# A two-layer hybrid encoder trunk on one core: fewer and larger residual loads, transposes placed earlier between matmuls, and a rolled vector loop

## The chip, the cores and the metric

The kernel runs on one core of one Trainium2 chip. The metric is the device time of one execution in microseconds (us). Engines are named as the profile names them: PE (TensorE), DVE (VectorE), ACT (ScalarE), POOL (GpSimd) and SP (SyncE, which issues most of the loads). PSUM is written by PE and read by DVE and ACT.

## The reference

512 tokens of width 2048 pass a layer of mixer A and a layer of mixer B. Only what the change touches is shown; the last line of each layer, a 512x2048 by 2048x2048 product with a residual added, is where most of the changed lines stand.

```python
def layer_a(h, ...):
    u = rms_norm(h, g_norm)
    x_rnn, g_rnn, q_mem, g_mem = jnp.split(u @ w_in, ...)
    x_rnn = causal_depthwise_conv(x_rnn, conv_w, conv_b)
    y_rnn = rg_lru(x_rnn, ...) * jax.nn.silu(g_rnn)      # three turns of four blocks of 128 channels
    y_mem = memory_attention(q_mem, mem_k, mem_v) * jax.nn.silu(g_mem)
    return h + jnp.concatenate([y_rnn, y_mem], axis=-1) @ w_out

h = layer_a(x, ...)
k_sb, v_sb = jnp.split(rms_norm(h, kv_norm) @ w_kv, 2, axis=-1)
h = layer_b(h, ..., k_sb, v_sb, ...)                      # same shape, stick-breaking attention
return rms_norm(h, final_norm)
```

## The kernel before, in words

Every large product runs in fp32r as three passes (`three_passes`, L1666 to L1668): each operand is split into a high part, made by ACT, and a low part, made by DVE as the difference, and PE multiplies high by high, high by low and low by high. So each piece of weights that lands in SBUF goes landing, ACT (`w_hi`), DVE (`w_lo`), PE, and each engine's order is written out by hand with counting semaphores.

**Output projections.** `project(s, ...)` computes layer s's output product by Strassen's scheme with seven block products per half: 28 "halves" (u = 0 to 27), each of 24 matmuls with 512 columns, each on 1 MB of weights (`load_proj` on SP's queue, `proj_split` on ACT and DVE). ACT splits the weights of half u once half u-2 is done. While SP's queue brings the weights, ACT's queue brings the residual: `load_resid` in layer A reads x in four loads of 512 columns (1 MB each, issued behind the splits of halves 4, 7, 10 and 13), `load_h2` in layer B reads h in four such loads and the final gain in a fifth (behind 4, 7, 10, 12 and 14). DVE adds the residual to the products as they come out of PSUM.

**Transposes of h.** The next product, with `w_kv`, wants h transposed. Eight units q of eight 128x128 transposes each (`h_transposed(q)` on PE, L1720) write two PSUM banks; `h_fill(q)` on ACT (L541) and then on DVE (L1026) copy them out as high and low parts, after which `h_lo` counts the banks free. `H_UNITS` says which columns unit q takes, `h_unit` which banks. Units 0 to 3 share two banks and stand before halves 20, 21, 22 and 23; unit 4 stands in half 27; units 5, 6 and 7 stand in the first two slabs of the next product. A slab is four tiles of twelve matmuls; a hook `{t: f}` runs f before tile t. Unit 5 uses other banks than unit 4.

**The recurrent loop.** Layer A's input projection runs in three turns of two groups of four slabs. PE, ACT and SP run it as a rolled loop (`Fori`), DVE unrolled. DVE's part of slot 0 and 1 is the convolution (L1353, L1359) and the low part of its result (L1373), for which PE waits with the gates. ACT stores y at slot 7 (`store_y`, L658); DVE waits for that store in slot 3 of the next turn before it overwrites the tile.

**The end.** The last quadrants of layer B's product are added (`last_sum`, L1627), squared on ACT (L952), and each row of four tiles is scaled: ACT scales the left half (`row_scale`, L981), DVE the right half (`row_out`), and SP stores them. For rows 0 and 1, `row_out` multiplies chunk 3 by the gain and the scale in one instruction; for rows 2 and 3 the gain has been multiplied in earlier (`pregain`, L1561).

Of the kernel before, what the change touches and what calls it, by code (L numbers as in the profile page):

```python
# [19 lines left out]
P = 128  # L20
# [4 lines left out]
C = 512  # L25
# [5 lines left out]
NPAIR = NB // 4  # L31
# [4 lines left out]
CONV = 4  # L36
# [16 lines left out]
F_MEM, F_X = 0, 4  # L53
H_UNITS = ((0, 0), (0, 1), (1, 0), (1, 1), (3, 0), (2, 0), (3, 1), (2, 1))

# [6 lines left out]
ALU = mybir.AluOpType  # L62
# [41 lines left out]
def trunk(nc, x, x_t, mem, mem_t, gain_cols, chan_cols, w_mem_kv, w_in_a, w_rec_gate, w_in_gate,  # L104
# [23 lines left out]
    with ExitStack() as ctx:  # L128
# [3 lines left out]
        def sem(name):  # L132
            return ctx.enter_context(nc.semaphore(name))
# [72 lines left out]
        def h_rows(q, t, k):  # L206

            c, second = H_UNITS[q]
            at = P * (2 * second + k)
            return r_a[c // 2][:, t, c % 2, at:at + P]  # L210

        def h_unit(q):

            k0 = 4 * H_UNITS[q][0] + 2 * H_UNITS[q][1]
            banks = main[:, 0:2, :] if q < 4 else aux[:, 2 * (q % 2):2 * (q % 2) + 2, :]
            return slice(k0, k0 + 2), banks

# [82 lines left out]
        y_stored = sem("y_stored")  # L300
        resid_loaded = [sem(f"resid_loaded{c}") for c in range(4)]
        h_stored = sem("h_stored")
# [214 lines left out]
        def _(act):  # L517
# [275 lines left out]

            def load_resid(m):
                act.wait_ge(y_stored, 64)
                act.dma_start(r_a[m // 2][:, :, m % 2, :], x_v[:, :, C * m:C * m + C]).then_inc(resid_loaded[m], 16)

# [4 lines left out]
            def late_a(u):  # L802
                if u == 16:
                    act.wait_ge(r_done, 2)
                    act.wait_ge(psum_read, 7)
                    act.dma_start(h_v[:, :, 0:2 * C], r_a[0][:].rearrange("p t c n -> p t (c n)")
                                  ).then_inc(h_stored, 16)
                if u in (18, 20):
                    for t in (u - 18, u - 17):
                        if t:  # L810
                            act.wait_ge(h_squares, t)
                        nc.scalar.activation(work[:, 0:1024], r_a[0][:, t], ACT.Square, accum_out=ss[:, t, 1:2]
                                             ).then_inc(h_squares, 1)
                if u == 21:
                    h_fill(0)
                if u == 22:
                    h_fill(1)
                if u == 23:
                    h_fill(2)
                if u == 24:  # L820
                    h_fill(3)
# [6 lines left out]

            project(0, late_a, load_resid, (4, 7, 10, 13))
            extra[0] = N_PROJ  # L830
            act.wait_ge(r_done, 3)
            store_h(3)
            split(G_KV, 0, g_kv)
            h_fill(4)
            for j in range(4):
                split_next(G_KV, j, g_kv, g_kv)
                if j == 0:
                    store_h(2)
                    h_fill(5)
                    h_fill(6)  # L840
                if j == 1:
                    h_fill(7)
                    chunk_squares(3, 1)
                    chunk_squares(2, 2)
                if j == 2:
                    root(3)
# [128 lines left out]

            project(1, late_b, load_h2, (4, 7, 10, 12, 14))

# [19 lines left out]
        def _(dve):  # L997
# [340 lines left out]
            for b in range(4):  # L1338
                branch_out(G_A, b)
            for i in range(NPAIR):  # L1340
                for q in range(2):
                    G = 2 * i + (G_A + 1 + q)
                    for j in range(4):
# [31 lines left out]
                        if slot == 3:  # L1375
                            if i:
                                dve.wait_ge(y_stored, 16 * i)
                            for b in range(4):
                                gate_out(G, b)
# [16 lines left out]
                        if slot == 7:  # L1396
                            for b in range(4):
                                branch_out(G, b)
            mem_branch(0, G_A + 7, g_a)

            r11, r12, r21, r22 = project(0, r_a, lambda n: dve.wait_ge(resid_loaded[n], 16))

            for u in range(16, N_PROJ):
# [6 lines left out]
                if u == 18:  # L1410
                    dve.wait_ge(resid_loaded[3], 16)
                    fifth(0, r22, r12)
                if u == 21:
                    h_fill(0)
                    dve.wait_ge(resid_loaded[2], 16)
                    first_copy(0, r11)
                if u == 22:
                    h_fill(1)
                if u == 23:
                    h_fill(2)  # L1420
                    y_quad(0, 16, q_k1[1], 2)
                if u == 24:
                    h_fill(3)
                    second_sums(0, aux[:, 2:4, :])
# [12 lines left out]
            V.tensor_tensor(r21, main[:, 2:4, :], r21, ALU.add).then_inc(psum_read, 1)  # L1437
            h_fill(4)

            for j in range(4):  # L1440
                split_next(G_KV, j, g_kv, g_kv)
                if j == 0:
                    h_fill(5)
                    h_fill(6)
                if j == 1:
                    h_fill(7)
                if j == 2:
                    dve.wait_ge(h_squares, 12)
                    mean_square(4, ss[:, :, 1:4])
                    rstd_rows(3)  # L1450
# [161 lines left out]
            ch.link(V.reduce_sum(mx[:], ss[:, :, 0:3], AX_X))  # L1612
            ch.link(V.tensor_scalar(mx[:], mx[:], 1.0 / D, EPS, ALU.mult, ALU.add))

            def row_out(t):
                o = h2[:, t, 3, :]
                if t < 2:
                    V.scalar_tensor_tensor(o, o, rstd[:, t:t + 1], fgain[:, 3 * C:4 * C], ALU.mult, ALU.mult)
                else:
                    V.tensor_scalar(o, o, rstd[:, t:t + 1], None, ALU.mult)  # L1620
                o = h2[:, t, 2, :]
                V.scalar_tensor_tensor(o, o, rstd[:, t:t + 1], fgain[:, 2 * C:3 * C], ALU.mult, ALU.mult
                                       ).then_inc(scaled[1], 1)
# [37 lines left out]
        def _(pe):  # L1661
# [44 lines left out]
            def h_transposed(q):  # L1706
# [6 lines left out]
                else:  # L1713
                    pe.wait_ge(r_done, 3)
                    pe.wait_ge(psum_read, 12 if H_UNITS[q][0] == 3 else 14)
                    if q > 5:
                        pe.wait_ge(h_lo, q - 1)
                for k in range(2):
# [173 lines left out]
            half(0, 20, a23, 2, 0)  # L1892
            h_transposed(1)
            half(0, 21, a23, 2, 1)
            h_transposed(2)
            pe.wait_ge(p1_copied, 2)
            half(0, 22, a01, 3, 0)
            h_transposed(3)
            half(0, 23, a01, 3, 1)
# [10 lines left out]
            for j in range(4):  # L1910
                hooks = {}
                if j == 0:
                    pe.wait_ge(psum_read, 13)
                    hooks = {2: lambda: (pe.wait_ge(psum_read, 14), h_transposed(5)), 3: lambda: h_transposed(6)}
                if j == 1:
                    hooks = {1: lambda: h_transposed(7)}
                if j == 2:
# [109 lines left out]
```

## Time and profile before

| | |
|---|---|
| median of 3 runs | 1490.51 us (1490.11 to 1491.57) |
| the profiled execution | 1490.51 us, of which the span of instructions is 1488.8 us |
| PE busy | 1474.2 us, 99% of the span |
| DVE, ACT busy | 928.1 us (62%), 682.6 us (46%) |
| granted TensorE clock | 0.998 |
| DMA | 314.90 MB, mean 212 GB/s |

The span runs from the first to the last instruction; 1.7 us of the time lie around it. A matmul's end in the trace is modelled, so two matmuls overlap in it; the time from one start to the next is what one costs.

### The profile page before, as it was taken

The numbers are of one execution on the slowest core, as the hardware profiler recorded it, in microseconds if no ns is written. First come the engines' busy times: TensorE is split into PE (matmuls) and PEld (weight loads), VectorE is DVE, ScalarE is ACT, GpSimd is POOL, SyncE is SP. The second block draws the span as 40 slices with busy tenths as digits, with TensorE's granted clock in tenths as the row PEclk, the third lists the DMA queues.
The fourth block names the chain that finished last, engine by engine and source line by source line (L and its number), as shares of the span: only waits on it lengthen the run. The fifth ranks groups of instructions, "written<-read, shape, count | busy, mean of one in ns | idle before, by whom it ended". The sixth has DMA issues, their size and how long they took to land.

```text
span 1488.8 us, 18103 instructions
## 1 busy us (share of the span) xinstructions
PE 1474.2 (99%) x6754; PEld 1225.9 (82%) x6754; DVE 928.1 (62%) x1319; ACT 682.6 (46%) x1087; POOL 93.4 (6%) x140
## 2 busy tenths in 40 slices
PE   8999999999999999999999999999999999999997
PEld 7888888888888888888888888888888888888886
DVE  5764568465677896843433334556666566678877
ACT  5764454445445545552323222433443433555465
POOL 0001111111110000011111101100000000000000
PEclk9999999999999999999999999999999999999999
DMA  9786788777786986378877998883342433349853
GB/s 325 245 337 215 160 217 226 179 228 156 206 251 181 334 301 245 137 258 223 244 205 215 293 212 248 231 204 123 140 142 86 141 138 127 130 167 343 309 196 141
DMA packets 157753, 314.90 MB, mean 212 GB/s; under 512 B 6656, under 2 KB 36352, under 8 KB 154624
## 3 DMA queue, kind: packets, MB, share of 16 engines
q1 hardware_dynamic: 103312, 197.06, 37.8%
q0 software_dynamic: 23040, 67.12, 20.8%
q10 hardware_dynamic: 31344, 49.98, 9.6%
q8 instruction: 34, 0.56, 0.1%
q14 instruction: 23, 0.19, 0.0%
HBM read 284.77 MB, written 96.47 MB: 256 GB/s over the span
## 4 chain that ended last, share of the span: by engine, by line
PE 93%; DMA 2%; DVE 2%; ACT 1%; issue 0%; SPq 0%; ACTq 0%; DVEq 0%
PE main L1666 25%; PE main L1667 25%; PE main L1668 25%; PE aux L1666 5%; PE aux L1667 5%; PE aux L1668 5%; PE aux L1958 2%; DMA w_raw<-weight_sums 1%; PE aux L1947 1%; DMA y_scratch<-work 1%; PE aux L1789 0%; DMA w_raw<-in_w_mem_kv 0%; DVE w_lo L1013 0%; ACT w_hi L527 0%; ACT work L554 0%; DVE work L1240 0%
## 5 line engine op out<-in xcount | busy, mean ns | idle before, releaser
L1013 DVE SCALAR_TENSOR_TENSOR w_lo<-w_raw,gains,w_hi 128x512 fp32r<-128x512 f32 x412 | 282.3, 746 | 311.6 <-ACT w_hi L527 311.1
L1666 PE MATMUL main<-act_hi,w_hi 128*128 128x512 f32 x1216 | 475.7, 391 | 0.0
L1668 PE MATMUL main<-act_hi,w_lo 128*128 128x512 f32 x1216 | 473.8, 390 | 0.0
L1667 PE MATMUL main<-act_lo,w_hi 128*128 128x512 f32 x1216 | 473.6, 389 | 0.0
L527 ACT ACTIVATE w_hi<-w_raw,gains 128x512 fp32r<-128x512 f32 x412 | 264.1, 714 | 384.4 <-PE main L1668 324.7
L1668 PEld LDWEIGHTS main<-act_hi,w_lo 128*128 128x128 f32 x1216 | 228.2, 188 | 48.1
L1667 PEld LDWEIGHTS main<-act_lo,w_hi 128*128 128x128 f32 x1216 | 228.4, 188 | 46.6
L1666 PEld LDWEIGHTS main<-act_hi,w_hi 128*128 128x128 f32 x1216 | 228.3, 188 | 46.4
L1666 PE MATMUL main<-w_hi,act_hi 128*128 128x512 f32 x544 | 212.5, 391 | 2.2 <-DVE w_lo L1122 1.9
L1668 PE MATMUL main<-w_hi,act_lo 128*128 128x512 f32 x544 | 211.8, 389 | 0.0
L1667 PE MATMUL main<-w_lo,act_hi 128*128 128x512 f32 x544 | 211.7, 389 | 0.0
L1666 PEld LDWEIGHTS main<-w_hi,act_hi 128*128 128x128 f32 x544 | 102.1, 188 | 25.4 <-DVE w_lo L1122 3.5
L1668 PEld LDWEIGHTS main<-w_hi,act_lo 128*128 128x128 f32 x544 | 102.1, 188 | 21.2
L1667 PEld LDWEIGHTS main<-w_lo,act_hi 128*128 128x128 f32 x544 | 102.1, 188 | 20.9
L562 ACT ACTIVATE w_hi<-w_raw 128x1024 fp32r<-128x1024 f32 x64 | 64.3, 1052 | 79.1 <-issue 62.2
L1043 DVE TENSOR_TENSOR w_lo<-w_raw,w_hi 128x1024 fp32r<-128x1024 f32 x64 | 75.6, 1221 | 38.1 <-ACT w_hi L562 38.0
L1666 PE MATMUL aux<-w_hi,act_hi 128*128 128x512 f32 x224 | 87.8, 392 | 0.6 <-DVE w_lo L1043 0.6
L1667 PE MATMUL aux<-w_lo,act_hi 128*128 128x512 f32 x224 | 87.2, 389 | 0.0
L1668 PE MATMUL aux<-w_hi,act_lo 128*128 128x512 f32 x224 | 87.2, 389 | 0.0
L562 ACT ACTIVATE w_hi<-work 128x1024 fp32r<-128x1024 f32 x48 | 48.2, 1053 | 53.5 <-issue 48.6
L494 POOL DMA_DIRECT2D weight_sums<-in_w_out_b x48 | 37.6, 787 | 458.1 <-issue 226.5
L1043 DVE TENSOR_TENSOR w_lo<-work,w_hi 128x1024 fp32r<-128x1024 f32 x48 | 56.6, 1220 | 14.3 <-ACT w_hi L562 14.1
(238 smaller groups left out, 1401.3 us busy)
## 6 DMA issues: line engine op xcount, KB each, us to landing
w_raw<-in_w_in_a SPq DMA_DIRECT2D x32, 1024.0 KB, 7.3
w_raw<-in_w_in_b SPq DMA_DIRECT2D x32, 1024.0 KB, 6.4
weight_sums<-in_w_out_a POOLq DMA_DIRECT2D x48, 512.0 KB, 7.4
w_raw<-in_w_kv SPq DMA_DIRECT2D x24, 1024.0 KB, 7.5
weight_sums<-in_w_out_b POOLq DMA_DIRECT2D x48, 512.0 KB, 7.6
w_raw<-weight_sums SPq DMA_DIRECT2D x18, 1024.0 KB, 8.2
weight_sums<-weight_sums POOLq DMA_DIRECT2D x32, 512.0 KB, 7.4
w_raw<-in_w_mem_kv SPq DMA_DIRECT2D x15, 1024.0 KB, 5.2
```

Of the source, the lines that this page charges most:

```text
L494: pool.dma_start(dst[rows], src[rows], accum_op=op).then_inc(sums_made[n], 16)
L527: nc.scalar.activation(w_hi[:, j % 2, k, :], w_raw[:, j % 2, k, :], ACT.Copy, scale=s).then_inc(hi_ready, 1)
L562: nc.scalar.activation(w_hi[:, u % 2, k:k + 2, :], proj_raw[RAW[u]][:, k:k + 2, :], ACT.Copy).then_inc(hi_ready, 2)
L1013: ins = V.scalar_tensor_tensor(lo, w_raw[:, j % 2, k, :], gain[:, KS * j + k:KS * j + k + 1], hi, ALU.mult, ALU.subtract)
L1043: V.tensor_tensor(w_lo[:, u % 2, k:k + 2, :], proj_raw[RAW[u]][:, k:k + 2, :], w_hi[:, u % 2, k:k + 2, :].bitcast(F32), ALU.subtract).then ...
L1666: TE.matmul(o, a[0], b[0], start=first, stop=False)
L1667: TE.matmul(o, a[0], b[1], start=False, stop=False)
L1668: return TE.matmul(o, a[1], b[0], start=False, stop=final)
L1947: last = TE.transpose(o, beta[:, t, c:c + P], ident[:])
L1958: last = TE.matmul(aux[:, 0, P * k:T], v, w, start=(k, n) == order[0], stop=(k, n) == order[-1])
```

## The change

It does six things. Unit q of the transposes takes the chunks in pairs (`CHUNK`), and unit 5 now writes the banks of unit 4, unit 6 the other two. On PE, unit 2 moves from before half 22 into the middle of half 21, unit 3 into the middle of half 22, unit 5 from tile 2 to tile 1 of the next product's first slab, unit 6 from tile 3 to tile 2, and unit 7 from tile 1 to tile 0 of the second; the fills follow. The fill of unit 4 moves behind the weight split of the next slab on ACT and on DVE. The residual x is read in two loads of 1024 columns (2 MB each), behind the splits of halves 4 and 5. The loads of h and the gain go out behind halves 4, 6, 8, 10 and 12. DVE's recurrent loop is rolled, with the wait for the y store at the end of slot 7 of the same turn. At the end, the gain of chunk 3 of rows 0 and 1 is multiplied in beforehand by two more instructions.

```diff
@@ -51,7 +51,7 @@
...
 F_MEM, F_X = 0, 4
-H_UNITS = ((0, 0), (0, 1), (1, 0), (1, 1), (3, 0), (2, 0), (3, 1), (2, 1))
+CHUNK = (0, 0, 1, 1, 3, 3, 2, 2)
@@ -205,15 +205,16 @@
...
-            c, second = H_UNITS[q]
-            at = P * (2 * second + k)
+            c = CHUNK[q]
+            at = P * (2 * (q % 2) + k)
             return r_a[c // 2][:, t, c % 2, at:at + P]
...
-            k0 = 4 * H_UNITS[q][0] + 2 * H_UNITS[q][1]
-            banks = main[:, 0:2, :] if q < 4 else aux[:, 2 * (q % 2):2 * (q % 2) + 2, :]
-            return slice(k0, k0 + 2), banks
+            k0 = 4 * CHUNK[q] + 2 * (q % 2)
+            banks = (main, main, main, main, aux, aux, aux, aux)[q]
+            b = (0, 0, 0, 0, 0, 0, 2, 0)[q]
+            return slice(k0, k0 + 2), banks[:, b:b + 2, :]
@@ -298,7 +299,7 @@
...
         y_stored = sem("y_stored")
-        resid_loaded = [sem(f"resid_loaded{c}") for c in range(4)]
+        resid_loaded = [sem("resid_loaded0"), sem("resid_loaded1")]
         h_stored = sem("h_stored")
@@ -791,9 +792,10 @@
...
-            def load_resid(m):
+            def load_resid(n):
                 act.wait_ge(y_stored, 64)
-                act.dma_start(r_a[m // 2][:, :, m % 2, :], x_v[:, :, C * m:C * m + C]).then_inc(resid_loaded[m], 16)
+                act.dma_start(r_a[n][:].rearrange("p t c n -> p t (c n)"), x_v[:, :, 2 * C * n:2 * C * n + 2 * C]
+                              ).then_inc(resid_loaded[n], 16)
@@ -815,9 +817,8 @@
...
                     h_fill(1)
+                    h_fill(2)
                 if u == 23:
-                    h_fill(2)
-                if u == 24:
                     h_fill(3)
@@ -826,16 +827,16 @@
...
-            project(0, late_a, load_resid, (4, 7, 10, 13))
+            project(0, late_a, load_resid, (4, 5))
             extra[0] = N_PROJ
...
             split(G_KV, 0, g_kv)
-            h_fill(4)
             for j in range(4):
...
                     store_h(2)
+                    h_fill(4)
                     h_fill(5)
@@ -973,7 +974,7 @@
...
-            project(1, late_b, load_h2, (4, 7, 10, 12, 14))
+            project(1, late_b, load_h2, (4, 6, 8, 10, 12))
@@ -1337,7 +1338,8 @@
...
                 branch_out(G_A, b)
-            for i in range(NPAIR):
+            with dve.Fori(0, NPAIR) as i:
+                ch.enter(i, 2 * (2 + 2 * (CONV - 2)) + 2 + 6)
                 for q in range(2):
@@ -1373,8 +1375,6 @@
...
                         if slot == 3:
-                            if i:
-                                dve.wait_ge(y_stored, 16 * i)
                             for b in range(4):
@@ -1396,9 +1396,11 @@
...
                                 branch_out(G, b)
+                            dve.wait_ge(y_stored, 16 * i + 16)
+                ch.leave(NPAIR)
             mem_branch(0, G_A + 7, g_a)
-            r11, r12, r21, r22 = project(0, r_a, lambda n: dve.wait_ge(resid_loaded[n], 16))
+            r11, r12, r21, r22 = project(0, r_a, lambda n: dve.wait_ge(resid_loaded[0], 16))
@@ -1408,19 +1410,18 @@
...
                 if u == 18:
-                    dve.wait_ge(resid_loaded[3], 16)
+                    dve.wait_ge(resid_loaded[1], 16)
                     fifth(0, r22, r12)
...
                     h_fill(0)
-                    dve.wait_ge(resid_loaded[2], 16)
                     first_copy(0, r11)
...
                     h_fill(1)
+                    h_fill(2)
                 if u == 23:
-                    h_fill(2)
                     y_quad(0, 16, q_k1[1], 2)
+                    h_fill(3)
                 if u == 24:
-                    h_fill(3)
                     second_sums(0, aux[:, 2:4, :])
@@ -1435,11 +1436,11 @@
...
             V.tensor_tensor(r21, main[:, 2:4, :], r21, ALU.add).then_inc(psum_read, 1)
-            h_fill(4)
...
                 if j == 0:
+                    h_fill(4)
                     h_fill(5)
@@ -1611,13 +1612,12 @@
...
             ch.link(V.tensor_scalar(mx[:], mx[:], 1.0 / D, EPS, ALU.mult, ALU.add))
+            pregain(3, 0)
+            pregain(3, 1)
...
                 o = h2[:, t, 3, :]
-                if t < 2:
-                    V.scalar_tensor_tensor(o, o, rstd[:, t:t + 1], fgain[:, 3 * C:4 * C], ALU.mult, ALU.mult)
-                else:
-                    V.tensor_scalar(o, o, rstd[:, t:t + 1], None, ALU.mult)
+                V.tensor_scalar(o, o, rstd[:, t:t + 1], None, ALU.mult)
                 o = h2[:, t, 2, :]
@@ -1712,9 +1712,9 @@
...
                     pe.wait_ge(r_done, 3)
-                    pe.wait_ge(psum_read, 12 if H_UNITS[q][0] == 3 else 14)
-                    if q > 5:
-                        pe.wait_ge(h_lo, q - 1)
+                    pe.wait_ge(psum_read, 12 if q < 6 else 14)
+                    if q > 4:
+                        pe.wait_ge(h_lo, (5, 0, 6)[q - 5])
                 for k in range(2):
@@ -1890,12 +1890,9 @@
...
             half(0, 20, a23, 2, 0)
-            h_transposed(1)
-            half(0, 21, a23, 2, 1)
-            h_transposed(2)
+            half(0, 21, a23, 2, 1, lambda t: h_transposed(1 + t))
             pe.wait_ge(p1_copied, 2)
-            half(0, 22, a01, 3, 0)
-            h_transposed(3)
+            half(0, 22, a01, 3, 0, lambda t: h_transposed(3) if t else None)
             half(0, 23, a01, 3, 1)
@@ -1911,9 +1908,10 @@
...
                     pe.wait_ge(psum_read, 13)
-                    hooks = {2: lambda: (pe.wait_ge(psum_read, 14), h_transposed(5)), 3: lambda: h_transposed(6)}
+                    hooks = {1: lambda: h_transposed(5),
+                             2: lambda: (pe.wait_ge(psum_read, 14), h_transposed(6))}
                 if j == 1:
-                    hooks = {1: lambda: h_transposed(7)}
+                    hooks = {0: lambda: h_transposed(7)}
                 if j == 2:
```

## Rows read from the trace of the kernel before

**Rows 1.** The page: busy us, share of the span, instructions.
```profile
PE 1474.2 (99%) x6754; PEld 1225.9 (82%) x6754; DVE 928.1 (62%) x1319; ACT 682.6 (46%) x1087; POOL 93.4 (6%) x140
```

**Rows 2.** Chain that ended last, us 494 to 510: start, us, what.
```profile
495.94 9.15 DMA w_raw<-weight_sums
...
506.38 1.24 DVE w_lo L1043
...
507.66 0.50 PE aux L1666
```

**Rows 3.** SP's and ACT's issues, by time: start, us, engine, line.
```profile
496.48 0.53 SPq L422 DMA_DIRECT2D work<-in_w_out_a  x1
...
498.02 0.39 ACTq L796 DMA_DIRECT2D work<-in_x  x1
```

**Rows 4.** DMA, us 496.4 to 496.8: issues, KB each, us to landing.
```profile
work<-in_w_out_a SPq DMA_DIRECT2D x1, 1024.0 KB, 13.1
```

**Rows 5.** DMA queues, us 502 to 508: packets, MB, share of 16 engines.
```profile
q1 hardware_dynamic: 672, 1.32, 58.6%
q10 hardware_dynamic: 520, 1.03, 45.2%
```

**Rows 6.** DMA queues, us 1393 to 1395.
```profile
q10 hardware_dynamic: 244, 0.50, 66.0%
q1 hardware_dynamic: 248, 0.25, 36.5%
```

**Rows 7.** DMA queues, us 564 to 571: a store of 4 KB rows on q10.
```profile
q10 hardware_dynamic: 523, 2.08, 74.9%
```

**Rows 8.** Chain, us 586 to 660: the transposes.
```profile
595.95 0.87 PE main L1720 x8
...
602.29 0.87 PE main L1720 x8
...
634.20 0.87 PE aux L1720 x8
```

**Rows 9.** ACT and DVE by time, around the second fill.
```profile
597.95 1.01 ACT L541 ACTIVATE act_hi<-main 128x1024 fp32r<-128x1024 f32 x1
...
599.50 1.22 DVE L1026 TENSOR_TENSOR act_lo<-main,act_hi 128x1024 fp32r<-128x1024 f32 x1
```

**Rows 10.** DVE by time, around the fifth fill.
```profile
637.86 1.23 DVE L1437 TENSOR_TENSOR work<-main,work 128x1024 f32<-128x1024 f32 x1 [2.85 <-PE main L1668]
...
640.13 2.73 DVE L1013 SCALAR_TENSOR_TENSOR w_lo<-w_raw,gains,w_hi 128x512 fp32r<-128x512 f32 x4
```

**Rows 11.** ACT, DVE, PE by time, around the loop's third turn.
```profile
322.05 0.41 ACTq L658 DMA_DIRECT2D y_scratch<-work  x1
...
330.96 2.74 DVE L1013 SCALAR_TENSOR_TENSOR w_lo<-w_raw,gains,w_hi 128x512 fp32r<-128x512 f32 x4 [1.44 <-ACT w_hi L527]
...
339.64 1.28 DVE L1373 TENSOR_TENSOR xc_lo<-work,xc_hi 128x512 fp32r<-128x512 f32 x2
...
342.23 0.40 PE L1666 MATMUL aux<-xc_hi,gate_hi 128*128 128x512 f32 x1
```

**Rows 12.** DMA, us 322 to 322.5: issue, KB, us to landing.
```profile
y_scratch<-work ACTq DMA_DIRECT2D x1, 1024.0 KB, 9.5
```

**Rows 13.** DVE and ACT by time, at the end.
```profile
1468.38 1.28 DVE L1561 TENSOR_TENSOR work<-work 128x512 f32<-128x512 f32 x2
...
1476.20 0.68 DVE L1627 TENSOR_TENSOR work<-main,work 128x512 f32<-128x512 f32 x1
...
1479.82 0.69 DVE L1627 TENSOR_TENSOR work<-main,work 128x512 f32<-128x512 f32 x1 [0.79 <-PE main L1668]
...
1474.87 2.19 ACT L981 ACTIVATE work<-work,rstd 128x1024 f32<-128x1024 f32 x2 [1.03 <-DVE rstd L1648]
```

**Rows 14.** Stretches at the end: us, busy by engine, PEclk, DMA, GB/s.
```profile
1480.00:1483.70 3.70, 0.00 (x0) 0.00 (x0) 3.47 (x10) 2.38 (x5) 0.00 (x0) 1.00 1.02 402
1483.70:1488.80 5.10, 0.00 (x0) 0.00 (x0) 0.00 (x0) 0.00 (x0) 0.00 (x0) 0.50 0.71 283
```

## The prediction

> **What bounds the kernel now.** I read the page first: PE is busy for 1474.2 of the 1488.8 us of the span [rows 1], so only 14.6 us are not PE's, most of them ahead of the first product and behind the last. I take from this that a change which only relieves another engine can save nothing worth measuring, and that each microsecond for which PE newly waits is a microsecond of the time. So the question for every edit is whether PE arrives somewhere before what it needs. I then read the chain that ended last around layer A's output projection. It leaves PE there: the load for half 5 is issued at 495.94 and lands 9.15 us later, at 505.09; DVE's first low part ends at 507.62 and PE starts half 5 at 507.66 [rows 2]. So from landing to PE it takes 2.57 us, and half 5 has no slack at all. I read the transposes in the chain too: unit 1 at 595.95, unit 2 at 602.29, each 0.87 long [rows 8], so a half takes 602.29 - 595.95 - 0.87 = 5.47 us and a tile, half of it, 2.73 us. Then the times of DVE and ACT around the fills, the DMA queues, and the end.
>
> **The two large loads of x: +3.2 us (0 to 4.4).** Half 6's weights are issued at 496.48 and land 13.1 us later, at 509.6 [rows 3, 4]. PE starts half 6 at 507.66 + 5.47 = 513.1 and needs them landed by 513.1 - 2.57 = 510.5, so half 6 has 0.9 us of slack. The first load of x is issued at 498.02 [rows 3]; between 502 and 508 its queue moves 1.03 MB, the whole 1 MB load, beside 1.32 MB of weights, 2.35 MB in 6 us or 0.39 MB/us together [rows 5]. So I place the start of its traffic at 502, 4 us behind its issue, and there the weights still lack, at half the rate, 0.195 x 3.1 = 0.60 MB of half 5's load.
>
> How do two queues share? Where q1 moved rows of 1 KB and q10 rows of 2 KB, the packets were equal in number, 248 and 244, and the bytes 0.25 and 0.50 MB [rows 6]. So the packet is what is shared. Rows of 2 KB go as packets of 2 KB (520 for 1.03 MB [rows 5]) and rows of 4 KB as packets of 4 KB (523 for 2.08 MB [rows 7]). The new loads of x have 4 KB rows against weights of 2 KB, so I give the weights one third, 0.13 MB/us, while x is loading, and x two thirds, 0.26.
>
> The first x load then lasts from 502 to 510 (2.1 MB / 0.26), and the second, issued behind the split of half 5, follows at once or, if it too needs 4 us from an issue at about 507, at 511. Half 5's weights land at 502 + 0.60 / 0.13 = 506.6, 1.5 us late, and PE waits those 1.5 us. Half 6's 1.05 MB take 8.1 us more, to 514.7, or with the gap of 0.9 us between the x loads at 0.39 MB/us 1.8 us less, to 512.9. Against 510.5 that is 2.4 to 4.2 us late in all; the wait of half 5 is contained in it. I take 3.2. Half 7 comes through even: x ends at about 518, the weights of half 7 then have their last 0.5 MB at the full rate and land at 519.2, and PE starts half 7 at 513.1 + 3.2 + 5.47 = 521.8, which is 519.2 + 2.57. If it misses, it misses by tenths (upper end 4.4). The lower end is the equal share by bytes: then half 5 is as before and half 6's load lands at 505.1 + 1.05 / 0.195 = 510.5, just in time, for 0. The later loads of x fall away, but no half waited for weights there, so that gives nothing back. DVE's new wait for the first x load, ahead of half 7's split, is met when the load lands at about 510.5.
>
> The Trainium skill bears on this (DMA: Bandwidth & Descriptors, the table of terms under SWDGE vs HWDGE vs iDMA): a packet is preferably at most 4096 B and holds up to 64 descriptors, and the engine changes queue at packet boundaries. If rows of 2 KB were bundled up to 4 KB, the two queues would share by bytes and the sum would lack this term; by the rows above it has it.
>
> **Unit 2's transposes: +1.1 us.** They must wait until DVE has read unit 1 out of the shared banks. Before, ACT copies unit 1 from 597.95 and DVE from 599.50 to 600.72, and PE comes at 602.29 with 1.6 us to spare [rows 8, 9]. Now PE comes after unit 1 and one tile, at 595.95 + 0.87 + 2.73 = 599.55. Nothing in front of the two copies has moved, since ACT's and DVE's weight splits still precede them, so PE waits until 600.7: 1.15 us. Queued behind PE's wait is the rest of half 21; ACT's next split waits for that half and shifts with it. Unit 3 needs unit 2's copies: transposes end at 601.6, ACT 1.0 and DVE 1.2 more, 603.9, against PE at 600.7 + 0.87 + 5.47 = 607.0. No wait.
>
> **Unit 5's transposes: +2.4 us.** They now use unit 4's banks and come a tile earlier. Unit 4 starts at 634.20 [rows 8]; with its 0.87 and a tile of 2.73 the next slab starts at 637.8, and PE reaches the new place one tile later, at 640.5. What it needs is DVE's copy of unit 4, and that now stands behind the weight split. DVE adds from 637.86 to 639.1, and its four splits take 2.73 us [rows 10], to 641.75; the copy takes 1.22 [rows 9], to 642.9. PE waits 2.4 us. Had the copy stayed in front of the split, it would be 640.3 and the wait nothing; the order is what costs. Unit 6 has its own banks, unit 7 comes 9 us later; the slab behind has all its weights.
>
> **The end: +0.5 us (0 to 1.25).** The two extra multiplications, 1.28 us for a pair [rows 13], stand on DVE ahead of the scale that both ACT's first row scales (2.19 us from 1474.87) and the first `last_sum` (1476.20) wait for. ACT squares the sum right behind its row scales, so it is up to 1.25 us late; DVE's idle 0.79 us before the last sum at 1479.82 [rows 13] takes most of it. 1.25 - 0.79 is about 0.5; the cheaper scaling of two tiles gives back two or three tenths at most, off ACT's path.
>
> **The rolled loop: 0.** The new wait bites once: the y store issued at 322.05 takes 9.5 us, to 331.5, and DVE's next split started at 330.96, so 0.6 us. It is covered, since DVE's low part of the first block ends at half of 1.28 behind 339.64, 340.3, and PE comes for it at 342.23 [rows 11, 12]: 1.9 us of slack. What is left of it, 1.3 us, must hold any cost of values in registers, over some fourteen instructions.
>
> **The earlier loads of h: 0.** They stay 1 MB with 2 KB rows, one per two halves (10.9 us). At 0.39 MB/us all together a pair of halves wants 2 MB of weights and 1 MB of h, 3.15 MB or 8.1 us. The first, which falls on the tight half 5, is where it was. If that is wrong, its price is some tenths.
>
> **Sum.** 3.2 + 1.1 + 2.4 + 0.5 = 7.2 us. The profiled execution took 1490.51 us, which is the median of the runs as well, so no correction: 1497.7 us.
>
> **The rivals.** *Share by bytes (0.18).* The large loads cost nothing and the sum is 1490.5 + 4.0 = 1494.5. For it: rows of equal size share equally, so [rows 5] alone can't tell; against it [rows 6]. *Not slower (0.08): the copies are early.* The price of both transposes hangs on PE standing ahead of DVE; it vanishes if ACT and DVE have copied unit 1 by 599.5 and unit 4 by 640.5. With x also sharing by bytes this gives 1490.5 + 0.5 = 1491.0. Against it is that each copy is behind a split on two engines, and that 2.4 us don't fit into spare time of tenths. *The clock falls (0.06).* A wait of PE lets the granted clock drop from 2.4 to 1.2 GHz. The only drop in view is after the end: PE's last product is done before 1479.82 and the clock is 0.50 from 1483.7 on, over 5.1 us [rows 13, 14]. My longest wait is 2.4 us, shorter than those 3.9. Were the clock low for as long as 5.1 us after one wait, it would cost half, 2.6 us: 1500.3. The Trainium skill (TensorE: Matmul & The Clock Gate, HAM oscillation) warns that a DMA wait between groups of matmuls lets the array throttle again; no row here shows it within the work. *The rolled loop costs PE (0.04).* If each of the fourteen instructions took 0.15 us more, 2.1 + 0.6 - 1.9 = 0.8 us a turn, 2.4 for three: 1500.1.
>
> **How the numbers follow.** My sum keeps 0.62; 0.02 is left for a gain that I don't see. A difference under 0.2%, 3 us, is about what can't be told from no change. Even by bytes the sum is 4 us over. Slower takes 0.62 + 0.18 + 0.06 + 0.04 = 0.90, same 0.08, faster 0.02. The range leaves out the not slower case: from 1493.5 (by bytes, with the end at nothing and half a microsecond off the waits) to 1500.3, the upper ends of the loads and the end, or the clock.
>
> **What would show it.** In PE's waits: halves 5 and 6 waiting on `w_lo` for about 1.5 and 1.7 us, unit 2's transposes on `act_lo` for 1.1 and unit 5's for 2.4. Half 6's load landing at 513 to 515, with twice as many bytes as weights on ACT's queue from 502 on. DVE's turn of the loop 0.6 us later once. I am wrong if half 6's load lands by 511, if the transposes start without a wait, or if some half between 7 and 14 waits because DVE does not catch up.

## The result

The changed kernel takes 1501.68 us in the median of 6 runs, against 1490.93 us for the kernel before (6 runs on the same chips): a ratio of 1.0083, 95% interval 1.0062 to 1.0103. It is slower, by 10.7 us, and outside the predicted range. Its runs also spread, from 1500.56 to 1508.97 us, where those of the kernel before lie within 1.5 us. The execution with the profile took 1507.18 us with a span of 1505.5, so it is near the upper end of them, and the account below is of that one: 16.7 us. The median is not the time of such a run: with the profiled one there are seven, four between 1500.56 and 1501.77 us and three at 1505.24, 1507.18 and 1508.97.

The page (busy us, share of the span, instructions), which answers to [rows 1]:

```profile
PE 1479.1 (98%) x6754; PEld 1228.4 (82%) x6754; DVE 929.4 (62%) x1321; ACT 682.7 (45%) x1087; POOL 93.3 (6%) x140
```

PE has the same 6754 matmuls and 5 us more of busy time for them; the other 12 us are idle, nearly all of it waits. PE's waits (who waited for whom: us in total, times, longest us):

```profile
PE aux L1666 <- DVE w_lo L1044: 4.1, 4, 2.2
PE aux L1666 <- DVE mv_lo L1191: 3.4, 2, 3.1
...
PE aux L1720 <- DVE act_lo L1027: 2.5, 1, 2.5
...
PE main L1720 <- DVE act_lo L1027: 1.3, 1, 1.3
```

Three of the four rows were forecast: the weights' low parts around halves 5 to 7 (3.5 of the 4.1 us; the rest is half 5 of layer B, which waited 0.4 us before too), and the transposes of units 5 and 2. The second was not: 3.1 us in one wait for `mv_lo`, at the first head of layer A's memory attention, right behind the recurrent loop. Before, that group was 0.2 us. DVE, ACT and PE around it, by time (start, us, engine, line; in brackets the idle time before and what ended it), with the landing of ACT's issue:

```profile
416.14 0.41 ACTq L659 DMA_DIRECT2D y_scratch<-work  x1
...
422.93 0.69 DVE L1163 TENSOR_TENSOR work<-main,rstd_bc 128x512 f32<-128x512 f32 x1 [2.03 <-PE main L1668]
...
427.23 0.69 DVE L1197 TENSOR_TENSOR q_lo<-work,q_hi 128x512 fp32r<-128x512 f32 x1 [3.61 <-DMA y_scratch<-work]
...
428.74 0.36 PE L1666 MATMUL aux<-mk_hi,q_hi 128*128 128x256 f32 x1 [3.13 <-DVE mv_lo L1191]
```

```profile
y_scratch<-work ACTq DMA_DIRECT2D x1, 1024.0 KB, 10.9
```

ACT issues the third turn's y store at 416.14. It lands 10.9 us later, at 427.0. DVE has finished the turn at 423.6 and stands at the new wait for that store; in the kernel before it went straight on to the low parts of the first head. PE, which had 0.6 us in hand there, comes for them at 425.6 and gets them at 428.74.

The clock shows what becomes of the waits (stretch, us, PE, PEld, DVE, ACT, POOL busy with their counts, PEclk, DMA, GB/s), and PE's matmuls in the first of these stretches:

```profile
429.30:432.70 3.40, 3.40 (x15) 3.01 (x14) 2.56 (x5) 0.04 (x1) 0.77 (x1) 0.50 0.14 25
...
432.70:436.00 3.30, 3.30 (x16) 2.70 (x15) 3.27 (x8) 2.51 (x10) 0.16 (x1) 1.00 0.63 78
...
654.60:658.00 3.40, 3.40 (x14) 2.92 (x12) 0.84 (x1) 1.02 (x1) 1.72 (x3) 0.50 1.07 331
...
658.00:661.00 3.00, 3.00 (x19) 2.55 (x18) 0.38 (x1) 0.28 (x1) 0.00 (x0) 1.00 0.81 272
```

```profile
431.38 0.63 PE L1667 MATMUL main<-act_lo,w_hi 128*128 128x512 f32 x1
431.81 0.63 PE L1668 MATMUL main<-act_hi,w_lo 128*128 128x512 f32 x1
```

Twice the granted clock is at half, 1.2 GHz, for 3.4 us: from 429.3, behind the wait of 3.1 us, and from 654.6, behind unit 5's wait of 2.5 us. At half clock a matmul of 512 columns follows the last after 0.43 us, at the full 2.4 GHz after 0.23; so each fall costs half of 3.4, 1.7 us. The kernel before has no such stretch inside the work.

So the 16.7 us are: waits for weights 3.5, unit 2 1.3, unit 5 2.5, the memory head 3.1, two falls of the clock 3.4, the end 0.9, together 14.7. The rest is small: 0.8 us in the loop, 0.6 from first loads that land later, and the slower first matmul behind each wait.

### The profile page after: what moved, and what is told of

It is laid out like the page before. It is cut to its first block, busy times and chain, and to the rows that moved or that the text cites. A ratio compares the mean times of both kernels' runs of the same rounds, so it can differ in the third digit from the quotient of the medians.

```text
span 1505.5 us, 18338 instructions
## 1 busy us (share of the span) xinstructions
PE 1479.1 (98%) x6754; PEld 1228.4 (82%) x6754; DVE 929.4 (62%) x1321; ACT 682.7 (45%) x1087; POOL 93.3 (6%) x140
## 4 chain that ended last, share of the span: by engine, by line
PE 85%; DVE 6%; DMA 5%; ACT 2%; issue 1%; SPq 0%; DVEq 0%; ACTq 0%
PE main L1666 23%; PE main L1667 23%; PE main L1668 23%; PE aux L1666 4%; PE aux L1667 4%; PE aux L1668 4%; DMA y_scratch<-work 2%; PE aux L1956 2%; DMA work<-weight_sums 2%; DVE w_lo L1014 1%; DMA w_raw<-in_w_mem_kv 1%; PE aux L1945 1%; DVE w_lo L1044 1%; DMA w_raw<-weight_sums 1%; ACT w_hi L528 0%
```

## The experiments

Kernels named "changed" start from the changed kernel, the others from the kernel before. Each was timed in five rounds beside the kernel before. Medians are given with lowest and highest. The kernel before had medians of 1490.3 to 1490.6 us there.

**1. The loop as before (changed kernel).**

```diff
-            with dve.Fori(0, NPAIR) as i:
-                ch.enter(i, 2 * (2 + 2 * (CONV - 2)) + 2 + 6)
+            for i in range(NPAIR):
...
                         if slot == 3:
+                            if i:
+                                dve.wait_ge(y_stored, 16 * i)
...
-                            dve.wait_ge(y_stored, 16 * i + 16)
-                ch.leave(NPAIR)
```

> The changed kernel with DVE's recurrent loop as it was: unrolled, and the wait for the y store back in slot 3 of the next turn. Theory: what the prediction missed is the wait at the end of the third turn, where PE lost 3.3 us at the first memory head and then 3.4 us at half the clock (1.7 us). Then the PE wait on mv_lo (3.4 us in the changed kernel's profile) is 0.2 us as before, the clock drop behind it is gone, the two small gate waits of 0.3 us go as well, and the time is near the predicted 1497.7 us plus the 1.7 us of the second clock drop: 1498 to 1500, with a spread between runs below 2 us, where the changed kernel's was 8. Rival: the loss comes from somewhere else and this changes less than 1 us.

Measured: 1501.88 us (1501.25 to 1503.62), ratio 1.0077 (1.0064 to 1.0090). The wait on `mv_lo` is back at 0.2 us although this execution's third store took 9.2 us to land, and the spread is 2.4 us in place of 8.4. The median didn't fall: it was expected at 1498 to 1500 and is 1501.88, as the changed kernel's 1501.68. So the loop's change isn't what puts the changed kernel's median above the forecast; it makes the long runs. In this kernel's profile PE waits 3.5 us before halves 5 to 7, 1.3 and 2.5 us for units 2 and 5, the clock falls once (1.7 us), and the end is 1.2 us longer: 10.2 us. A load that landed late near 65 us, with a wait of 1.4 us, is why the profiled execution, 1503.21, is above the median. Why the median is about 2 us above what I expected isn't shown.

**2. The loop unrolled, with the late wait (changed kernel).** As experiment 1, but only the loop's head is put back; the wait stays at the end of slot 7.

```diff
-            with dve.Fori(0, NPAIR) as i:
-                ch.enter(i, 2 * (2 + 2 * (CONV - 2)) + 2 + 6)
+            for i in range(NPAIR):
...
-                ch.leave(NPAIR)
```

> The changed kernel with the loop unrolled again but the wait for the y store left at the end of slot 7. Theory (the wait's place is the cause): as the changed kernel, 1500 to 1507 us with a wide spread, DVE waiting on the y store in turns in which it lands late, PE waiting for mv_lo by up to 3 us. Rival (rolling the loop is the cause: values in registers, the branch): as the loop put back whole, 1498 to 1500, no wait on mv_lo.

Measured: 1507.36 us (1501.38 to 1510.22), ratio 1.0113 (1.0098 to 1.0128). The spread is back, 8.8 us, with the loop unrolled. So it goes with the wait's place and not with the rolling. The median is high because three of five runs are long ones, against three of seven of the changed kernel; the quickest runs are 1501.38 and 1500.56. The execution with the profile happened to be the quickest: its third store landed in 5.2 us, and PE's wait on `mv_lo` was 0.2. Its clock fell once, behind unit 5's wait (the two stretches with it):

```profile
647.00:650.00 3.00, 1.68 (x9) 1.71 (x10) 1.18 (x2) 0.00 (x0) 0.90 (x2) 0.74 0.96 295
650.00:653.00 3.00, 3.00 (x11) 2.40 (x11) 1.23 (x1) 1.02 (x1) 0.82 (x2) 0.69 1.01 323
```

This execution, 0.3 us below the changed kernel's median, shows what a run without the late store is made of: waits of 3.4 us before halves 5 to 7, 1.3 for unit 2, 2.5 for unit 5, 1.7 for the clock and 1.2 at the end are 10.1 of the 10.9 us by which its span is longer.

**9. The late wait alone (kernel before).**

```diff
                         if slot == 3:
-                            if i:
-                                dve.wait_ge(y_stored, 16 * i)
...
                                 branch_out(G, b)
+                            dve.wait_ge(y_stored, 16 * i + 16)
```

> The kernel before with only the wait for the y store moved from slot 3 of the next turn to the end of slot 7, the loop still unrolled. Theory: DVE waits for the store whenever it lands later than about 7 us after its issue in the third turn; a landing of 5.2 us costs nothing, one of 10 us about 2.4 us and one of 11 us 3.3 us of PE, plus 1.7 us if the clock falls. So 1490.6 us in the quickest run and up to 1497 in the slowest, a spread of several us where the kernel before has below 2. Rival (the spread of the changed kernel has another source): 1490 to 1492 in every run.

Measured: 1491.01 us over 12 runs (1489.79 to 1497.58), ratio 1.0013 (1.0001 to 1.0026). Nine runs lie between 1489.8 and 1493.0 and three at 1497.0, 1497.6 and 1497.6, which is 7 us more. The profile is of a quick run, with a landing of 5.1 us. None of the 35 runs of the kernel before beside it took more than 1494.4. So the wait alone makes the two kinds of runs. How the 7 us come about isn't shown: of this kernel's three long runs there is no trace, and the most that a trace of another kernel prices is the 3.1 us of wait and 1.7 of clock above, 4.8 us. One of the three, 1496.96, has a mean granted clock of 0.998, as the quick ones.

Over all profiled executions, the store of the third turn took 5.1 to 12.5 us to land. In the six kernels with the late wait, landing and PE's wait go together: 5.1, 5.1 and 5.2 us with 0.2 us at most, 9.3 with 1.5, 10.0 with 2.2, 10.9 with 3.1. Two of them, PE by time in experiments 3 and 4:

```profile
427.33 0.36 PE L1666 MATMUL aux<-mk_hi,q_hi 128*128 128x256 f32 x1 [2.20 <-DVE mv_lo L1190]
```

```profile
425.72 0.36 PE L1666 MATMUL aux<-mk_hi,q_hi 128*128 128x256 f32 x1 [1.51 <-DVE mv_lo L1190]
```

With the wait in slot 3 the landings were as scattered (5.2 to 12.5 us in eight executions) and PE's wait never above 0.2. From landing minus wait, the cover is 7.8 us.

**3. x in four loads (changed kernel).**

```diff
-            def load_resid(n):
+            def load_resid(m):
                 act.wait_ge(y_stored, 64)
-                act.dma_start(r_a[n][:].rearrange("p t c n -> p t (c n)"), x_v[:, :, 2 * C * n:2 * C * n + 2 * C]
-                              ).then_inc(resid_loaded[n], 16)
+                act.dma_start(r_a[m // 2][:, :, m % 2, :], x_v[:, :, C * m:C * m + C]).then_inc(resid_loaded[m], 16)
...
-            project(0, late_a, load_resid, (4, 5))
+            project(0, late_a, load_resid, (4, 7, 10, 13))
```

The semaphores and DVE's waits for the loads go back with it.

> The changed kernel with the residual x in four loads of 2 KB rows behind halves 4, 7, 10 and 13, as before. Theory: PE's waits for w_lo of halves 5, 6 and 7 (0.3, 2.2 and 1.0 us) go back to 0.4 us in all, and the time is 3.7 us below the changed kernel's for the same y store. Rival (the waits are covered by something behind them): less than 1 us.

Measured: 1501.70 us (1496.39 to 1506.10), ratio 1.0076 (1.0055 to 1.0096). The median can't be used, since the late wait is still in and its draw decides more than the loads; the quickest run is 4.2 us below the changed kernel's quickest. In the profile PE doesn't wait for halves 5 to 7 of layer A any more; the 0.5 us on `w_lo` that are left are half 5 of layer B. So the waits go, and the time is better read from experiment 7.

**7. The two loads of x alone (kernel before).** The reverse of experiment 3's edit.

> The kernel before with the two loads of x of 2 MB and 4 KB rows behind halves 4 and 5 alone. PE waits 1.2, 2.3 and up to 1 us before halves 5, 6 and 7 where the kernel before waits 0.3 in all: 3.7 us, 1494.3 us, or 1496.0 if the clock falls behind them. Rival (a wait here is taken back later, where DVE and DMA have slack): within 1 us of the kernel before.

Measured: 1494.94 us (1494.31 to 1496.71), ratio 1.0031 (1.0020 to 1.0042): 4.3 us. PE waits 2.1 us before half 5, 0.2 before half 6 and 0.9 before half 7. The sum, 3.2, is near that of the changed kernel (0.4, 2.2, 0.9 there), the distribution isn't: x is issued 1.2 us behind half 5's load here and 1.9 us behind it there. Over the five profiled executions with the large loads the waits add up to 2.2 to 3.5 us. The rest of the 4.3 us isn't assigned.

**4. The same burst with rows of 2 KB (changed kernel).** Experiment 3's loads, but two behind half 4 and two behind half 5.

```diff
-            project(0, late_a, load_resid, (4, 5))
+            project(0, late_a, lambda n: (load_resid(2 * n), load_resid(2 * n + 1)), (4, 5))
```

> The changed kernel with the same 4 MB of x behind the same halves 4 and 5, but in four loads of 1 MB with 2 KB rows, two behind each half. Theory (queues share by packets, so the row's length decides): weights and x get half each, half 6's load lands at about 15 us after its issue's start of sharing instead of 16.7 from issue, that is 13.5 to 14.5 us from its issue, and PE's waits there fall from 3.7 us to 0 to 1 us. Rival (the amount of data in the burst decides, whatever the rows): as the changed kernel, waits of 3.5 us and more.

Measured: 1498.18 us (1495.43 to 1505.77), ratio 1.0068 (1.0047 to 1.0089). PE's one wait for weights in this projection is 0.2 us, at 525.8, before half 8. The queues (packets, MB, share of 16 engines), first the changed kernel from 510 to 524 us with 4 KB rows, then this one from 506 to 520 with 2 KB rows:

```profile
q10 hardware_dynamic: 929, 3.69, 66.2%
q1 hardware_dynamic: 981, 1.96, 36.9%
```

```profile
q1 hardware_dynamic: 1359, 2.72, 52.4%
q10 hardware_dynamic: 1361, 2.70, 52.2%
```

Packets are equal in number in both, within 6%. Bytes are 1.96 against 3.69 MB in the one and 2.72 against 2.70 in the other. The same 4 MB of x at the same places cost 3.5 us of PE with long rows and 0.2 with short ones, so the amount isn't what decides. The edit also makes four loads of two; that the row's length is what counts, and not the number of loads, is read from the packets.

**6. The transposes alone (kernel before).** `CHUNK`, the banks, the places on PE and the order of the copies as in the change; loop, loads and end as before.

> The kernel before with the new order of the transposes and their copies alone; loop, loads and end as before. The sum by the changed kernel's waits is 1.3 + 2.5 = 3.8 us, and up to 1.7 us for each time the clock falls behind one of them: 1494.4 to 1497.8 us, a mean granted clock of 0.998 without such a fall, 0.997 with one. Rival (the waits of the changed kernel come only with the delays ahead of them): below 1493.

Measured: 1495.06 us (1493.65 to 1497.87), ratio 1.0029 (1.0017 to 1.0041): 4.5 us for 3.8 us of waits. The profile shows the waits at 1.3 and 2.5 us, and in it the clock falls once behind the second. The lowest run is 3.8 us above the lowest of the kernel before, just the waits. The profiled execution is this kernel's longest, 1497.87: it also has a wait of 1.4 us near 65 us that the edit has nothing to do with.

**5. Unit 4's copy in front of the split (changed kernel).** On ACT and on DVE:

```diff
             split(G_KV, 0, g_kv)
+            h_fill(4)
             for j in range(4):
                 split_next(G_KV, j, g_kv, g_kv)
                 if j == 0:
                     store_h(2)
-                    h_fill(4)
```

> The changed kernel with the copy of unit 4 put back in front of the next slab's weight split on ACT and DVE; nothing else. Theory (the order on DVE makes unit 5's transposes wait): PE's wait there falls from 2.5 us to under 0.3 us and the clock never falls behind it, so the time is 2.5 to 4.2 us below the changed kernel's for the same y store. Rival (using unit 4's banks a tile earlier is what costs): the wait stays above 1 us.

Measured: 1498.94 us (1496.80 to 1505.02), ratio 1.0071 (1.0056 to 1.0086). Unit 5's wait isn't among PE's waits at all: the banks and the earlier place cost nothing, the order of copy and split on ACT and DVE costs all of it. The lowest run is 3.8 us below the changed kernel's. The clock fell in this execution too, from 516.1 to 519.5, this time behind the wait of 2.2 us for half 6:

```profile
516.10:519.50 3.40, 3.40 (x10) 2.63 (x9) 3.02 (x3) 0.10 (x1) 0.00 (x0) 0.50 1.05 396
```

**8. The end alone (kernel before).**

```diff
             ch.link(V.tensor_scalar(mx[:], mx[:], 1.0 / D, EPS, ALU.mult, ALU.add))
+            pregain(3, 0)
+            pregain(3, 1)
...
-                if t < 2:
-                    V.scalar_tensor_tensor(o, o, rstd[:, t:t + 1], fgain[:, 3 * C:4 * C], ALU.mult, ALU.mult)
-                else:
-                    V.tensor_scalar(o, o, rstd[:, t:t + 1], None, ALU.mult)
+                V.tensor_scalar(o, o, rstd[:, t:t + 1], None, ALU.mult)
```

> The kernel before with the two extra gain multiplications ahead of the first row scales alone. By the prediction's step 0.5 us slower, between 0 and 1.25: the last product to the end of the span takes 9.1 us before and 9.6 to 10.3 us now. Rival (the cheaper scaling gives it back): no longer than 9.2 us.

Measured: 1491.58 us (1491.11 to 1492.98), ratio 1.0006 (0.9997 to 1.0015). The interval includes no change, the median is 1.0 us up, and from PE's last matmul to the end of the span it takes 10.7 us in the trace where it took 9.5. DVE and ACT at the end (experiment 8, by time):

```profile
1481.34 0.69 DVE L1626 TENSOR_TENSOR work<-main,work 128x512 f32<-128x512 f32 x1
...
1481.34 1.15 ACT L981 ACTIVATE work<-work,rstd 128x1024 f32<-128x1024 f32 x1 [0.87 <-DVE rstd L1636]
...
1482.39 0.61 ACT L952 ACTIVATE work<-work 128x512 f32<-128x512 f32 x1
```

DVE's 0.79 us ahead of its last sum [rows 13] are gone; the sum is done at 1482.0, but ACT squares it at 1482.39, behind the row scale that now starts together with the sum.

**10. The loads of h alone (kernel before).**

```diff
-            project(1, late_b, load_h2, (4, 7, 10, 12, 14))
+            project(1, late_b, load_h2, (4, 6, 8, 10, 12))
```

> The kernel before with the loads of h and the gain in layer B behind halves 4, 6, 8, 10 and 12 alone. By the prediction's step nothing: within 0.7 us of the kernel before, PE's only wait in that projection the one of 0.6 us before half 5. Rival (the denser loads delay weights): a new wait of PE between halves 7 and 14 of layer B.

Measured: 1490.57 us (1489.77 to 1492.64), ratio 1.0003 (0.9994 to 1.0011). No difference that the interval shows, as forecast.

**11. Three parts mended (changed kernel).** Experiments 1, 3 and 5 together; unit 2, the end and the loads of h stay changed.

> The changed kernel with the loop as before, x in four loads behind halves 4, 7, 10 and 13, and unit 4's copy in front of the split. What remains is unit 2's wait (1.3 us), the end (1.0 us) and the loads of h (0): 1492.9 us, 1492 to 1494, with a spread below 2 us and no clock drop before the end. Rival (the parts' costs don't add, something is left that no part shows): 1495 and more.

Measured: 1492.71 us (1492.05 to 1493.42), ratio 1.0016 (1.0007 to 1.0025), 2.4 us over the kernel before in this comparison, where the parts left in, unit 2 with 1.3 and the end with 1.0, add up to 2.3. PE's only new wait is unit 2's, 1.3 us, and the spread is 1.4 us. So the three parts taken out carry 8.3 of the 10.7 us, and the spread.

**12. The first residual load behind half 5 (kernel before).**

```diff
-            project(0, late_a, load_resid, (4, 7, 10, 13))
+            project(0, late_a, load_resid, (5, 7, 10, 13))
...
-            project(1, late_b, load_h2, (4, 7, 10, 12, 14))
+            project(1, late_b, load_h2, (5, 7, 10, 12, 14))
```

> The kernel before with the first residual load of each layer behind half 5 in place of half 4. The load then shares the queues no longer with the weights of half 5, for which PE waits 0.3 us in layer A and 0.6 in layer B. Theory: both waits go, 0.5 to 0.9 us faster, 1489.7 to 1490.1. Rival: DVE now waits for the residual ahead of half 7's split and PE waits there instead, no gain or a loss of up to 1 us.

Measured: 1489.30 us over 11 runs (1489.05 to 1490.41), ratio 0.9994 (0.9985 to 1.0002). PE's waits (who, total us, times, longest) have no row for the output projections any more:

```profile
PE main L1666 <- DVE w_lo L1122: 1.0, 1, 1.0
...
PE main L1666 <- DVE w_lo L1013: 0.2, 1, 0.2
```

The kernel before waited 0.2 us before half 5 of layer A and 0.4 in layer B (the expectation says 0.3 and 0.6). So these 0.6 us of waits are gone and the median is 1.0 us down, but the interval still holds no change. It is the best version found, and a gain of 0.06% isn't established by these runs.

## Why the prediction was wrong

The direction was right; the measured median is 4.0 us above the forecast and 1.4 us above the range. Two things that the sum took at nothing failed: the clock, which is the largest single part of the miss in the median, and the loop, which makes the long runs.

**The step that failed for the median is the one that left the clock out of the sum**: "My longest wait is 2.4 us, shorter than those 3.9", which held *the clock falls* at 0.06. The 3.9 us are those after which the clock fell at the end [rows 13, 14]. It fell inside the work behind waits of 3.1, 2.5 and 2.2 us. Behind unit 5's same 2.5 us it fell in four of the six profiled executions that had this wait, and not in those of experiments 3 and 4; behind the 2.2 us before half 6 it fell in one of four. So at these lengths it can go either way. The price was right in kind and less in size: 1.7 us a fall, not 2.6. In the run nearest the median that has a trace (experiment 2, 10.9 us longer) the clock makes 1.7 of the 3.7 us by which it exceeds the 7.2 us of the sum, the end 0.7, the three groups of waits 0.5, and 0.8 are not assigned. It isn't the whole miss: the changed kernel's fastest run, 1500.56, has a mean granted clock of 0.998, as the kernel before, and is still 0.3 us above the range. The other three quick runs have 0.995 or 0.996. The Trainium skill's warning (TensorE: Matmul & The Clock Gate, HAM oscillation), that a wait for data between groups of matmuls lets the array throttle again, is borne out here, by the rows with 0.50.

**The step that failed for the spread is "The rolled loop: 0"**, with its sentence that the new wait bites once. It counted the second turn's store alone, 9.5 us; the third turn's had landed in 5.2 us in that same execution, and so it dropped out, although the two figures already differed by 4 us. In the thirteen profiled executions of the changed kernel and of the experiments the third store took 5.1 to 12.5 us, and at the end of the third turn only 7.8 us are covered, because what follows there is the start of the memory attention, where PE has 0.6 us in hand, and not a convolution with 1.9. The wait costs nothing in one run and 7 us in another. It makes the spread; the median it moves by 0.7 us alone (experiment 9), and putting the loop back leaves it at 1501.88 (experiment 1). The rolling as such is cleared by experiment 2, as far as the spread goes; a rolled loop with the early wait wasn't tried.

**The two large loads of x: mechanism right, 3.2 forecast, 3.5 us of waits and 4.3 us alone.** The share by packets is as read: two thirds of the bytes to x. Half 5 was late by 0.4 us, not 1.5, although x's first packets came 3.9 us behind their issue, as forecast; in the four experiments that keep the large loads it waited 0 to 2.1 us, and why it varies isn't shown. Half 6's load took 16.7 us for a forecast of 16.4 to 18.2, and half 7, which I called even, waited 0.9. The rival share by bytes is excluded by the packets of experiment 4. The Trainium skill (DMA: Bandwidth & Descriptors, SWDGE vs HWDGE vs iDMA) gives a packet as preferably at most 4096 B and as the boundary at which the engine changes queue. Both fit these loads, whose packets were one row each, of 2 or 4 KB; that short rows are bundled up to 4 KB, the case that the prediction weighed, is not what the traces show.

**Unit 2: right, 1.1 forecast, 1.3 measured. Unit 5: right, 2.4 forecast, 2.5 measured**, and by the order of copy and split as argued (experiment 5). The rival that the copies are early is out.

**The end: mechanism right, size half.** I let DVE's idle 0.79 us absorb the delay. But ACT's chain takes it on: its next row scale starts as the sum does, and the square waits behind it. 1.0 us instead of 0.5 in the medians, 0.6 to 1.2 in the traces of the kernels that have this end.

**The loads of h: right, no difference shown.**

With the measured terms the sum is 3.5 + 1.3 + 2.5 + 1.0 = 8.3 us, and with one or two falls of the clock 10.0 to 11.7: 1500.5 to 1502.2, around the median. The medians of the parts alone say the same: 4.3 for the loads of x, 4.5 for the transposes (3.5 forecast), 1.0 for the end, 0.7 for the late wait and 0.2 for the loads of h add up to 10.7 us, which is what the whole change costs. Each of these figures is uncertain by 1 to 2 us, so that they meet so exactly is partly luck. What stays open is why the store's landing varies. POOL moves weight sums on its own queue at that time; in the changed kernel's profiled execution it moved 1.61 MB beside the store, in the kernel before 0.16 MB, but experiment 3 had a landing of 10.0 us beside 0.52 MB, so the amount alone doesn't explain it.

## What to carry to other kernels

Before a wait for a DMA is moved to where the engine's next work is urgent, ask for the longest landing in several executions, not for the one in the trace, and look at what stands behind the new place: here the second turn had 1.9 us in hand and the third 0.6. A change can then move the spread of the runs and hardly the median, so look at both. Where two queues loaded at once here, the one with longer rows took the larger share of the bytes, so prefetched data with long rows should not run beside weights with short ones that are due. In this kernel, at 99% of PE, waits of 2.2 to 3.1 us cost their own length and in some executions a stretch at half the clock on top.

## What the runs showed of the hardware

Two queues that loaded at once moved nearly equal numbers of packets, whatever their size: 981 and 929 with 2 and 4 KB, 1359 and 1361 with 2 KB each. The granted clock fell for 3.4 us behind waits as short as 2.2 us, in some executions and not in others. A 1 MB store from SBUF landed in 5.1 to 12.5 us at the same place of nearly the same program.
